# Last two experts' rows added by one-hot products, row gathers placed under the last expert stages, first experts run whole

## The reference

```python
grp = argmax(softmax(x @ w_rg + b_rg)); e_logits = (x @ w_re + b_re)[group grp]
top_v, top_i = lax.top_k(e_logits, 2)            # two experts of 32 per token
gate = softmax(top_v) * g_w
hdn = silu(xb @ w1[e]) * (xb @ w3[e])            # 1024 -> 512
y   = (hdn @ w2[e]) * w                          # 512 -> 1024
x   = layer_norm(DN_ALPHA * x + sum_of_y, ln2_g, ln2_b)
```

## Time and profile before

| | us |
|---|---|
| median of 3 runs | 3207.3 |
| the runs | 3198.17, 3207.3, 3210.28 |
| the profiled execution, its own time | 3200.73 |
| span of its trace | 3198.9 |
| PE busy | 3068.4 |
| DVE busy | 2159.2 |
| ACT busy | 1586.3 |
| POOL busy | 388.0 |

### The profile page before, as it was taken

How to read it: one execution, slowest core, us unless ns; L and a number is a source line. 1 busy time by engine, 2 the same in 40 slices (tenths; PEclk the granted TensorE clock), 3 DMA queues, 4 the chain that set the end, 5 groups by cost and what they waited for, 6 DMA issues and landing times.

```text
span 3198.9 us, 39413 instructions
## 1 busy us (share of the span) xinstructions
PE 3068.4 (96%) x14955; PEld 2380.4 (74%) x14955; DVE 2159.2 (67%) x2302; ACT 1586.3 (50%) x1905; POOL 388.0 (12%) x275
## 2 busy tenths in 40 slices
PE   8999899999989989899999989997999999999998
PEld 7668677777758868677777757877788888788887
DVE  3475788888863486788888865564476746767662
ACT  3572577777753272677777753442322213622211
POOL 0001222222220001232222230010100000000000
PEclk9999899999999998999999999999999999999999
DMA  7203699999972123799999973220223222232322
GB/s 273 110 1 132 262 360 360 351 361 361 356 264 79 37 70 154 298 347 355 356 353 362 358 223 87 59 53 1 85 87 106 89 108 93 86 110 82 106 93 79
DMA packets 174736, 600.47 MB, mean 188 GB/s; under 512 B 25537, under 2 KB 74865, under 8 KB 125203
## 3 DMA queue, kind: packets, MB, share of 16 engines
q1 hardware_dynamic: 140432, 541.22, 46.2%
q0 software_dynamic: 23680, 52.61, 4.7%
q10 hardware_dynamic: 10499, 4.91, 0.6%
HBM read 582.01 MB, written 48.23 MB: 197 GB/s over the span
## 4 chain that ended last, share of the span: by engine, by line
PE 81%; DVE 7%; DMA 6%; ACT 3%; issue 2%; POOL 1%; DVEq 0%; SPq 0%; ACTq 0%; POOLq 0%
PE bank L1947 20%; PE bank L1949 20%; PE bank L1948 20%; PE bank L1959 3%; PE bank L2617 2%; DMA ring<-w_gate 2%; PE bank L2341 1%; PE bank L2011 1%; PE bank L2012 1%; DMA expert_rows<-lnp 1%; PE bank L1954 1%; PE bank L1955 1%; PE bank L2306 1%; PE bank L2111 1%; DMA ring<-w_up 1%
## 5 line engine op out<-in xcount | busy, mean ns | idle before, releaser
L1948 PE MATMUL bank<-ring_rounded,big_rounded 128*96 128x512 f32 (+1 forms) x1768 | 694.9, 393 | 0.0
L3366 DVE TENSOR_TENSOR ring_rounded<-ring,big_rounded 128x2048 fp32r<-128x2048 f32 x252 | 567.5, 2288 | 38.3 <-ACT big_rounded L1388 36.8
L1388 ACT ACTIVATE big_rounded<-ring 128x2048 fp32r<-128x2048 f32 x252 | 478.5, 1918 | 62.7 <-DMA ring<-w_up 50.7
L2916 DVE TENSOR_TENSOR ring_rounded<-ring,ring_rounded 128x2048 fp32r<-128x2048 f32 (+2 forms) x118 | 260.4, 2246 | 334.3 <-ACT ring_rounded L1146 334.0
L1146 ACT ACTIVATE ring_rounded<-ring 128x2048 fp32r<-128x2048 f32 (+2 forms) x124 | 226.6, 1877 | 373.9 <-DMA ring<-ffn_w_down 152.5
L1947 PE MATMUL bank<-big_rounded 128*96 128x512 f32 x992 | 394.8, 398 | 1.6 <-DVE ring_rounded L3366 1.5
L1949 PE MATMUL bank<-big_rounded,XH_rounded 128*96 128x512 f32 x992 | 392.1, 395 | 0.0
L3366 DVE TENSOR_TENSOR ring_rounded<-ring,ring_rounded 128x2048 fp32r<-128x2048 f32 x128 | 292.7, 2288 | 146.9 <-ACT ring_rounded L1388 146.4
L1948 PEld LDWEIGHTS bank<-ring_rounded,big_rounded 128*96 128x96 f32 (+1 forms) x1768 | 294.0, 166 | 108.8
L1388 ACT ACTIVATE ring_rounded<-ring 128x2048 fp32r<-128x2048 f32 x128 | 245.1, 1916 | 220.5 <-DMA ring<-w_gate 220.4
L1947 PE MATMUL bank<-ring_rounded,big_rounded 128*96 128x512 f32 (+1 forms) x776 | 311.2, 401 | 9.5 <-DVE XH_rounded L3375 3.7
(11 more groups left out here) (487 smaller groups left out, 4922.8 us busy)
## 6 DMA issues: line engine op xcount, KB each, us to landing
ring<-w_up SPq DMA_DIRECT2D x128, 1024.0 KB, 7.9
ring<-w_down SPq DMA_DIRECT2D x128, 1024.0 KB, 8.0
ring<-w_gate SPq DMA_DIRECT2D x128, 1024.0 KB, 7.1
ring<-ffn_w_up SPq DMA_DIRECT2D x44, 1024.0 KB, 7.1
ring<-ret_gdn_w_in SPq DMA_DIRECT2D x8, 2048.0 KB, 13.0
ring<-ffn_w_down SPq DMA_DIRECT2D x8, 2048.0 KB, 7.8
expert_rows<-lnp POOLq DMA_DIRECT2D x1, 12288.0 KB, 41.7
ring<-odd_w_qkv SPq DMA_DIRECT2D x6, 2048.0 KB, 7.9
```

The lines of the kernel that those rows point to most:

```text
L1388: act.activation(one_pass(expert_hi(j)), expert_raw(j), ACT.Copy).then_inc(signal("half_rounded").sem, 1)
L1948: pe.matmul(dst, x_hi, y_lo, start=False, stop=False)
L2916: dve.tensor_tensor(one_pass(w), w, parts(hi(c)[:, ks, :]), ALU.subtract).then_inc(split[c.pair], 1)
L3366: dve.tensor_tensor(one_pass(expert_raw(j)), expert_raw(j), parts(expert_hi(j)), ALU.subtract).then_inc(signal("half_split").sem, 1)
```

## The change

1. `first_rows` on PE makes the rows of expert 0 untransposed (96x512, 4 products for each half of the tokens where there were 16), ACT and DVE copy them to SBUF, and PE transposes them with the ordinary `rows_T`.
2. Experts 0 and 1 are done whole: `stage_0` and `stage_1` run up, rows of the next, hidden and their own `down`. Expert 2's stage has no down part. From stage 3 on the order is as before.
3. In stages 3 to 6 DVE and PE also make one-hot matrices for experts 30 and 31 (`last_weights`, `mark_last`, `marks_T`), transposed, with a column of gate weights (`w_row`).
4. The rows of experts 30 and 31 are no longer scattered. ACT and DVE scale and split them (`last_rows`, `rest_of_rows`), and PE adds them into 8 PSUM tiles by 32 products (`last_rows`). DVE adds those to X (`add_last`).
5. `from_experts` waits only for the scatters up to expert 29, and gathers under stages 30 and 31: tile 0 as soon as these scatters have landed, tiles 1 to 3 behind `up(31)`. In layer 1 a transfer that waits for `up(31)` (the gain row) stands ahead of it in POOL's program, as before.
6. In the last stage `hidden_T(31)` stands between the halves of `down(30)`.
7. Fillers: 12 instead of 24 in layer 0, 20 in layer 1. Moments are written to a scrap tile; in layer 1 ACT's `moments` of tiles 2 and 3 stand one tile later.

```diff
-                with sp.Fori(1, EXPERTS - 1) as e:
+                next_down(1)
+                next_gate_up(1)
+                with sp.Fori(2, EXPERTS - 1) as e:
                     next_gate_up(e)
                     next_down(e)
...
-                scatter(EXPERTS - 2)
-                scatter(EXPERTS - 1)
...
                 for half in range(2):
-                    pool.wait_ge(signal(f"y_stored{half}").sem, 16 * (EXPERTS // 2) * (l + 1))
+                    pool.wait_ge(signal(f"y_stored{half}").sem, 16 * (EXPERTS // 2 - 1) * (l + 1))
+                pool.wait_ge(full[1], U[f"moe{l}"][1] + EXPERTS)
                 for t in range(T):
-                    for j, dst in enumerate((XH[:, t, :], M["YG"][:, t, :])):
+                    if t == 1:
+                        pool.wait_ge(full[3], U[f"moe{l}"][3] + EXPERTS)
+                    for j, dst in enumerate(rows_back[l][t]):
...
+            def moments(l, t):
+
+                for u in U[f"last{l}"][2 * t:2 * t + 2]:
+                    act.wait_ge(drained[u.bank], u.n + 1)
+                act.activation(tail_junk, X[:, t, :], ACT.Copy, accum_out=ssq[:, 16 + t:17 + t]).then_inc(act_done.sem, 1)
...
+                def first_rows():
+
+                    u = U[f"rows{l}"][0]
+                    act.wait_ge(full[u.bank], u.n + 1)
+                    act.activation(M["XE"][0:CAP, 0, 0:BANK], ps(u)[0:CAP, :], ACT.Copy).then_inc(drained[u.bank], 1)
+
+                def stage_0():
+                    silu(0, 0)
+                    rows_T(1, 1)
+                    hidden_T(0, 0)
+                    for j in GATE + UP[0:1]:
+                        round_half(1, j)
+                    out_rows(0, 0, 0, l > 0)
+                    round_half(1, UP[1])
+
+                def stage_1():
+                    round_half(1, DOWN[0])
+                    silu(1, 1)
+                    round_half(1, DOWN[1])
+                    round_half(2, GATE[0])
+                    rows_T(2, 0)
+                    hidden_T(1, 1)
+                    round_half(2, GATE[1])
+                    round_half(2, UP[0])
+                    out_rows(1, 1, 0, l > 0)
+                    round_half(2, UP[1])
+
...
-                stage(0, 0, 0, first=True)
-                stage(1, 1, 0, checked=l > 0)
-                stage(2, 0, 1, checked=l > 0)
-                with act.Fori(1, EXPERTS // 2 - 2) as i:
+                stage_0()
+                stage_1()
+                stage(2, 0, 1, down=False)
+                for i in (1, 2):
...
+                moments(1, 0)
+                moments(1, 1)
                 for t in range(T):
                     act.wait_ge(signal("x_normed").sem, signal("x_normed").next(act))
-                    act.activation(XH[:, t, :], X[:, t, :], ACT.Square, accum_out=ssq[:, t:t + 1]).then_inc(signal("x_ssq").sem, 1)
+                    act.activation(tail_junk, X[:, t, :], ACT.Square, accum_out=ssq[:, t:t + 1]).then_inc(signal("x_ssq").sem, 1)
                     act.wait_ge(signal("x_ssq").sem, signal("x_ssq").next(act))
                     if t:
                         rounded_tile("rms0_T", t - 1)
-                    if t + 2 < T:
-                        moments(t + 2)
+                    if 0 < t < T - 1:
+                        moments(1, t + 1)
                 rounded_tile("rms0_T", T - 1)
...
-            def first_chunk_by_tile(name, turned, src, told, lo_at):
-                keep_warm(U[turned][0], 24)
+            def first_chunk_by_tile(name, turned, src, told, lo_at, fillers):
+                keep_warm(U[turned][0], fillers)
...
                 pe.wait_ge(signal("first_marked").sem, signal("first_marked").next(pe))
-                for b in range(2):
-                    if q == 0:
-                        pe.wait_ge(drained[b], U[f"moe{l}"][b])
+                for h, u in enumerate(U[f"rows{l}"]):
+                    if q == 0 and u.n:
+                        pe.wait_ge(drained[u.bank], u.n)
                     for t in (2 * q, 2 * q + 1):
-                        x = X[:, t, :].rearrange("c (h p k) -> c h k p", h=2, k=4)
-                        for j in range(4):
-                            ins = pe.matmul(psum[b][:, j * CAP:(j + 1) * CAP], x[:, b, j, :], M["sel"][:, t, :],
-                                            start=(t == 0 and j == 0), stop=(t == T - 1 and j == 3))
+                        ins = pe.matmul(ps(u)[0:CAP, :], M["sel"][:, t, :], X[:, t, h * BANK:(h + 1) * BANK], start=(t == 0), stop=(t == T - 1))
                     if q == 1:
-                        ins.then_inc(full[b], 1)
...
+                def marks_T(i):
+                    pe.wait_ge(signal("first_marked").sem, signal("first_marked").next(pe))
+                    u = U[f"sel{l}"][i]
+                    if u.n:
+                        pe.wait_ge(drained[u.bank], u.n)
+                    for t in range(T):
+                        ins = pe.transpose(ps(u)[0:CAP, t * P:(t + 1) * P], M["sel_last"][:, t // 2, t % 2, 0:CAP], ident)
+                    ins.then_inc(full[u.bank], 1)
+
+                def hidden_T(e, half, marked=None):
                     wait_use(drained, 3, e, 1)
                     wait_use(drained, 4, e)
+                    if marked is not None:
+                        marks_T(marked)
+                        for t in range(T):
+                            pe.matmul(psum[4][0:CAP, KE * CAP:KE * CAP + 1], M["sel_last"][:, t // 2, t % 2, 0:CAP], w_last[:, marked, t:t + 1],
+                                      start=(t == 0), stop=(t == T - 1))
                     for kk in range(KE):
                         ins = pe.transpose(psum[4][:, kk * CAP:(kk + 1) * CAP], M["hid"][0:CAP, half, :].rearrange("c (h p k) -> c h k p", h=2, k=2)[:, kk // 2, kk % 2, :], ident[0:CAP, 0:CAP])
                     ins.then_inc(full[4], 1)
...
+                def stage_0():
+                    rows_T(0, 0, 0, first=True)
+                    up(0, 0, first=True)
+                    rows_T(1, 1, 0)
+                    hidden_T(0, 0)
+                    down(0, 0, early=True)
+
+                def stage_1():
+                    up(1, 1, early=True)
+                    rows_T(2, 0, 1)
+                    hidden_T(1, 1)
+                    down(1, 1, early=True)
+
+                def stage(e, half, n, early=False, last=False, marked=None):
+                    up(e, half, early=early)
                     if not last:
                         rows_T(e + 1, 1 - half, n + half)
-                    if not first:
+                    if last:
+                        down(e - 1, 1 - half, between=lambda: hidden_T(e, half))
+                        return
+                    if not early:
                         down(e - 1, 1 - half)
-                    hidden_T(e, half)
-
-                stage(0, 0, 0, first=True)
-                with pe.Fori(0, EXPERTS // 2 - 1) as i:
+                    hidden_T(e, half, marked)
+
+                def last_rows(t, i):
+                    for h in range(2):
+                        u = U[f"last{l}"][2 * t + h]
+                        n = slice(h * BANK, (h + 1) * BANK)
+                        if i == 0:
+                            pe.wait_ge(drained[u.bank], u.n)
+                        wait_use(drained, 5 + h, LAST[i], 1)
+                        for b in range(2):
+                            ins = pe.matmul(ps(u)[:, :], one_pass(M["selT"][0:CAP, i, t * P:(t + 1) * P]), one_pass(M["Y"][0:CAP, i, b, n]),
+                                            start=(i + b == 0), stop=(i + b == 2))
+                        if i == 1:
+                            ins.then_inc(full[u.bank], 1)
...
-                first_chunk_by_tile("qkv", "ln20_T", X, "x_normed", feature_rows(x_lo_T))
+                first_chunk_by_tile("qkv", "ln20_T", X, "x_normed", feature_rows(x_lo_T), 12)
...
-                first_chunk_by_tile("mix_in", "rms0_T", XH, "xh_ready", None)
+                first_chunk_by_tile("mix_in", "rms0_T", XH, "xh_ready", None, 20)
...
+                def stage_0():
+                    first_rows()
+                    rows_T(0, 0)
+                    dve.wait_ge(signal("scatter_issued").sem, signal("scatter_issued").next(dve))
+                    for j in GATE + UP + DOWN[0:1]:
+                        rest_of_half(0, j, early=True)
+                    hidden(0, 0)
+                    rest_of_half(0, DOWN[1], early=True)
+                    rows_T(1, 1)
+                    hidden_T(0, 0)
+                    for j in GATE + UP:
+                        rest_of_half(1, j, early=True)
+
...
+                def mark_last(i):
+                    if i == 1:
+                        wait_use(full, 4, 4)
+                    for t in range(T):
+                        ins = dve.tensor_scalar(M["sel_last"][:, t // 2, t % 2, 0:CAP], k("places"), pos_last[:, i, t:t + 1],
```

(34 more changed lines are left out.)

211 lines of the change are left out of this document (144 added, 67 removed).

## The result

The changed kernel took 3221.4 us (median of 6 runs, 3208.8 to 3225.5), the kernel before 3205.7 us (6 runs). The ratio is 1.0052 with a 95% interval of 1.0037 to 1.0066: 0.5% slower, 16.7 us of 3205.7 by the ratio (the medians are 15.7 apart). I had forecast 3212, with 3190 to 3227 for 8 in 10.

A forecast was written before the change was run, and what follows sets the result against it. It took PE's own work to bound the middle, with gains only at each expert part's ends. Heads -3.4, marks +5, tails -2.8 and +9.5 sum to +8.3 us; added to the mean 3204.1: 3212, 3190 to 3227 for 8 in 10.

The forecast's parts named there:

- layer 1's tail: Behind the last expert of layer 1: PE restarts 3.5 us behind T; loss 9.5 us with the load, bounds 5 and 14.
- First rows: Start of each layer's experts: fewer, wider products bring the first product of up(0) net 3.3 us earlier.
- Two whole experts: First stages: idle ahead of down(0), down(1) and up(3) of 3, 2.5 and 4 us; costs 1.6 us a layer.
- Marks: Stages 3 to 6: PE's extra transposes and tiny products cost between nothing and 6.4 us in all; 5 taken.
- The tail of layer 0: Behind the last expert of layer 0: 5.8 us gained behind T, 3 lost by a later T; net -2.8 us.
- T: End of the last expert's products in a layer; in the kernel before, 929.46 in layer 0 and 1874.82 in layer 1.
- The step on load against gathers: Ahead of down(31): gathers delay the last w_down load, 3 us taken of 0 to 5.2 in layer 0, 1 in layer 1.
- The circle: Layer 1's tail: rounding of tile 1 waits through other engines for DVE's rest(0); 14.2 us a tile for tiles 1 and 2.
- The middle: Middle of the experts: PE's own work, 18.06 us from one stage's transposes to the next's; nothing in the change shortens it.
- The first stages didn't fill the old idle stretch: Faster rival, 0.18: down(0) wholly fills the 7.29 us idle stretch, each layer gains 5.5; 3198, or 3193 with marks hidden.
- layer 1's tail didn't run like layer 0's: Rival, 0.2: add_last(2) comes early enough in layer 1's tail, so +9.5 turns to about -4; 3199.
- clock and load: Slower rival, 0.2: new idle stretches bring the half clock, and gathers take 5.2 us in both layers; 3224.

The follow-up runs named there:

- p_before: The kernel before, unchanged, profiled once more: 3205.0 us, ratio 1.0000.
- x4_marks4: The changed kernel with PE's marks four times (16 transposes and 16 tiny products instead of 4 and 4, twice a layer): 3236.9 us, ratio 1.0102.
- b1_rows: The kernel before with only the new first rows of the change: 3196.1 us, ratio 0.9981.
- x1_order: The changed kernel with layer 1's tail reordered: add_last and moments of tiles 2 and 3 earlier: 3212.6 us, ratio 1.0034.
- x6_oldstart: The changed kernel with the first stages in the order of before: 3215.8 us, ratio 1.0042.
- x8_oldrows: The changed kernel with the first rows as before: 3231.5 us, ratio 1.0077.
- x3_hold: The changed kernel with the gathers of tiles 1 to 3 held until the last product of expert 31: 3224.0 us, ratio 1.0059.
- x5_release: The changed kernel with expert 30's rows scaled and split ahead of rounding and splitting expert 31's second half of w_down: 3221.8 us, ratio 1.0059.
- y1_tails: The changed kernel with both tails reordered, fewer fillers, gathers of tiles 1 to 3 held and the order of x5_release: 3201.3 us, ratio 0.9991.
- x9_quiet: x3_hold with SyncE's loads of the next matrix's chunks also held until expert 31's last product, in both layers: 3229.9 us, ratio 1.0084.

## Why the prediction came out as it did

Direction and range held; the sum of +8.3 us was half of the 16.7 measured. That 3221.4 lies within the range is owed to its width as well: layer 1's tail, the largest term, came out at its upper bound of 14 or beyond it.

**First rows.** Right in mechanism, a little small. I had 3.3 us a layer; at the first product of up(0) the trace shows 3.6, and at the transposes ahead of stage 4 it is 4.4 by the table of windows.

**Two whole experts.** The three idle stretches came where I put them, 2.88, 1.72 and 3.48 for 3, 2.5 and 4. The term was too small: 1.6 us a layer against 3.6 in the table. Since both terms of the head were too small and have opposite signs, their sum came out nearer than they did: -1.7 a layer forecast, -0.8 measured. I had put 1.2 GHz behind the idle stretches into a rival and not into the sum. In layer 0 31 products at 0.43 instead of 0.23 us are 6.2 us, where the single old stretch had 11 such products behind it; the kernel before had 7 more at the head of up(0), where the changed kernel has none. In layer 1 there are 8, 0 and 9 behind the three stretches (2.88, 1.77, 3.58 us), where it was 5, and 13 in p_before. The Trainium skill (TensorE: Matmul & The Clock Gate, section on the clock gate) says that an idle PE falls to the half rate; five of these six stretches agree, and behind the 1.77 us of layer 1 every product ran at 0.23.

**Marks.** 5 taken, 5.2 by x4_marks4: right.

**The tail of layer 0.** -2.8 forecast, -0.4 measured: T comes 1.6 us later (I took 3), and the stretch behind it is 2.0 shorter (I took 5.8). What I left out are the 2.49 us of issue ahead of the last rows, where the kernel before had none; with records at 1.2 GHz behind them the last rows end at T + 11.7 where I had T + 7.7, and tile 0's products start at T + 24.7 where I had T + 21. From there to the end it is 28.6 us, as forecast (28.5). Over more executions even the 2.0 us of gain go: the stretch behind T takes 54.4 us on the mean in the kernel before (twice) and b1_rows, and 54.7 (53.2 to 58.8) in the changed kernel and the four variants with the same tail in layer 0 (x1_order, x4_marks4, x6_oldstart, x8_oldrows).

The step on load against gathers was right in kind, but small, and the mechanism of most of the wait was another. ACT takes up the second half of w_down 10.4 us after the issue of the pair (913.49, 923.85), where it was 9.1 and in p_before 8.9. But PE's 3.88 us ahead of down(31) end with DVE's L3557, the row that frees the PSUM bank, which stands on DVE behind that half, and 2.67 of them come from the new order alone (x3_hold). x5_release took the wait to 1.45 without touching a transfer.

**The tail of layer 1.** The term that failed in size: 9.5 forecast, 2.0 + 14.6 = 16.6 measured. The circle was right in place and nearly in size (13.2 us a step for 14.2), and x1_order took it away. The step that failed is that PE restarts 3.5 us behind T, as before, which I kept. It waits 4.00 and then 3.85 us, and with products at 1.2 GHz in between the last rows end at T + 18.0 instead of T + 10.9. These 7.1 us, with the shorter steps of the circle taken off (2.0) and the later T (1.0 more than I took), make up 6.1 of the 7.1 us that the term was short by. The pair of traces puts the term rather high: from T to the chunk's end it is 62.0 to 62.6 us in the three executions with the tail of before, and 76.8, 76.4, 73.8 and 71.9 in the changed kernel, x6_oldstart, x4_marks4 and x8_oldrows, which have the same tail. That is 12.4 on the means, and with T 1.3 later 13.7.

**The middle.** "PE's own work, and nothing in the change shortens it" holds for its floor only: 25 stages of 18.06 us are 451.5 us, and the executions took 455 to 470. By the mean over 22 values the changed kernels lose some 5 us a layer more there than those in the order of before; one set of marks (1.3 us) is in it. The terms above sum to 20 us without this by the pair of traces, and to 19 by the means over the executions; the measured 16.7 has an interval of 12 to 21, so the times leave little room for it. Whether the change slows the middle stays open.

**The rivals.** The first stages didn't fill the old idle stretch; layer 1's tail didn't run like layer 0's. The slower one, clock and load, had 3224 and was nearest in its number. Of its two causes the clock is in the rows, half-rate products behind most of the new idle stretches. The gathers' 5.2 us in both layers are not: T is 1.6 and 2.0 us later by the pair, 1.3 on the mean. What stood in their place are the issue stretches, which it didn't name.

## What to carry to other kernels

- When a tail is written for four tiles on three engines, follow one tile's chain through each engine's program order: one operation that is queued an item too late closed a circle that cost 6 us for each of two tiles. Moving operations, holding gathers back and dropping fillers, with the computation unchanged, turned 0.5% slower into no difference (y1_tails).
- Test the parts of a change alone, and compare them by a short window between two landmarks. Here the first rows were worth 4.4 us a layer and the reordering of the first experts cost 3.6, which the whole times hardly resolve; without the reordering and with reordered tails the change gives 0.37%.
- A wait that one removes doesn't shorten the whole if PE waits for something else just behind it: x5_release brought T 2.7 and 1.4 us earlier and left the time where it was. And read one wait in several variants before giving it a cause: the 2.67 us ahead of down(31) looked like the gathers' doing until x1_order showed the same.

## What the runs showed of the hardware

I hadn't expected the idle stretches marked issue where PE passes the code of a branch that isn't taken. Whether the first of them is there goes with the DMA engines' load. The 14 traces have 28 such places. At five of them the DMA share in the 3 us ahead of T was 0.20 or less (layer 0 of the kernel before in both of its traces, layer 0 of x3_hold, both layers of x9_quiet), and the first stretch was 0.00 at all five. At the other 23 the share was 0.69 to 1.05, and PE idled 1.6 to 6.7 us, 2.0 to 4.3 in layer 0. (The 1.58 us of p_before's layer 1 are put down to a row of ACT.) Two of the quiet places, in the kernel before and in x3_hold (stretch, length, busy by engine, PEclk, DMA share, GB/s):

```profile
926.46:929.46 3.00, 3.00 (x14) 2.01 (x13) 0.00 (x0) 0.59 (x1) 0.00 (x0) 1.00 0.14 48
```

```profile
932.60:935.60 3.00, 3.00 (x14) 1.92 (x12) 0.40 (x1) 0.69 (x1) 0.00 (x0) 1.00 0.14 46
```

How long the stretch gets doesn't follow from the share: it was 2.46 us at 1.01 (x8_oldrows, layer 1) and 6.71 at 1.02 (x5_release, layer 1). The page shows instruction transfers in queues of their own, q8 and q14. That PE waits there for its own instructions behind bulk transfers fits all of this, x9_quiet above all, but no row ties one such transfer to one stretch.

The second is the price of short idle stretches, and that it varies: in layer 0, behind 8.1 us of them in the first stages, stand 31 products at 1.2 GHz, which take 6.2 us more than at full clock; in layer 1, behind 8.2 us, there are 17, for 3.4 us.
